# Two transformer blocks on one core: a new order of tables, a sixth place for weights, and the last expert's rows

## What is computed

```python
def first_block(x, p, positions, ...):
    h = x
    for i in range(DEPTH):                      # 2
        u = h @ w_in[i]
        y_mla = mla_mixer(...)                  # latent attention, rotary angles from positions
        y_diff = diff_mixer(...)                # softmax(q1 k1 + bias) - lam * softmax(q2 k2 + bias)
        y_sb = sb_mixer(...)
        h = layer_norm(ALPHA * h + concat(y_mla, y_diff, y_sb) @ w_o[i])
        ffn = grouped_moe(h, ...)               # 16 experts, two per token
        ple = sigmoid(h @ ple_gate[i]) * (p[i] @ ple_proj[i])
        h = layer_norm(ALPHA * h + ffn + ple)
    return h

def grouped_moe(h, ...):
    for e in range(16):
        hid = silu(h @ w_gate[e]) * (h @ w_up[e])
        out = out + gate[..., e:e + 1] * (hid @ w_down[e])

def diff_mixer(...):
    lam = exp(sum(lq1 * lk1)) - exp(sum(lq2 * lk2)) + lam_init
    bias = rel_bias[t5_bucket(rel)]             # from the distance of positions, 4 heads
    ...
```

## Time and profile before

| | before |
|---|---|
| runs | 2003.84 us median of 3 (2003.21 to 2006.06) |
| the profiled execution | 2008.08 us, its span 2006.8 us |
| mean granted clock of TensorE | 0.962 |
| busy share | PE 91%, weight load 78%, DVE 68%, ACT 57%, POOL 9% |
| chain that ended last | PE 67%, DVE 20%, ACT 6%, issue 2%, DMA 1% |
| bytes moved | 413.17 MB, mean 206 GB/s |

### The profile page before, as it was taken

The page is one execution under the profiler, slowest core; times in us unless marked ns, Lnnn a source line. Parts: engine busy times, 40 slices in busy tenths (PEclk is TensorE's granted clock), DMA queues, the critical chain, the costliest instruction groups (busy, mean ns, idle before and its releaser), DMA issues.

```text
span 2006.8 us, 27459 instructions
## 1 busy us (share of the span) xinstructions
PE 1825.2 (91%) x11220; PEld 1572.5 (78%) x11220; DVE 1363.4 (68%) x1591; ACT 1138.1 (57%) x1576; POOL 173.9 (9%) x152
## 2 busy tenths in 40 slices
PE   5978898999799889998878999989999999999998
PEld 4866777777587777776768889979898889988997
DVE  5576799899647579889875566565555556556555
ACT  4464588887636458878863644434444645434443
POOL 0000132311000003312110000000000000000000
PEclk9889899999889889999989999999999999999999
DMA  8314398999742348999884444645554544454552
GB/s 239 111 64 163 120 365 327 333 357 331 252 146 85 131 147 316 333 342 346 323 288 144 146 154 149 206 139 200 189 184 154 168 139 156 160 197 168 183 195 84
DMA packets 203011, 413.17 MB, mean 206 GB/s; under 512 B 16352, under 2 KB 118496, under 8 KB 186496
## 3 DMA queue, kind: packets, MB, share of 16 engines
q1 hardware_dynamic: 201792, 409.76, 59.2%
q10 hardware_dynamic: 1088, 1.57, 0.4%
HBM read 409.47 MB, written 1.84 MB: 205 GB/s over the span
## 4 chain that ended last, share of the span: by engine, by line
PE 67%; DVE 20%; ACT 6%; issue 2%; DMA 1%; POOL 0%; DVEq 0%; ACTq 0%
DVE weights_lo L389 12%; PE PS L404 9%; PE PS L408 9%; PE PS L405 9%; PE PS L412 7%; PE PS L415 6%; PE PS L416 6%; PE PS L1393 3%; PE PS L1396 3%; PE PS L1439 3%; PE PS L1418 3%; ACT weights_hi L384 2%; DMA arena<-in_w_down 1%; PE PS L1379 1%; DVE expert_rows_lo L1649 1%
## 5 line engine op out<-in xcount | busy, mean ns | idle before, releaser
L389 DVE TENSOR_TENSOR weights_lo<-weights_raw,weights_hi 128x1024 fp32r<-128x1024 f32 (+1 forms) x600 | 702.6, 1217 | 240.4 <-ACT weights_hi L384 238.0
L384 ACT ACTIVATE weights_hi<-weights_raw 128x1024 fp32r<-128x1024 f32 (+1 forms) x600 | 594.6, 1045 | 136.5 <-PE PS L416 84.4
L404 PE MATMUL PS<-hT_hi,weights_hi 128*128 128x256 f32 (+1 forms) x1488 | 428.6, 288 | 20.3 <-ACT weights_hi L384 11.4
L408 PE MATMUL PS<-hT_hi,weights_lo 128*128 128x256 f32 (+1 forms) x1488 | 425.8, 286 | 5.1 <-DVE weights_lo L389 5.1
L405 PE MATMUL PS<-hT_lo,weights_hi 128*128 128x256 f32 (+1 forms) x1488 | 425.4, 286 | 0.0
L404 PEld LDWEIGHTS PS<-hT_hi,weights_hi 128*128 128x128 f32 (+1 forms) x1488 | 285.9, 192 | 27.8 <-issue 14.5
L408 PEld LDWEIGHTS PS<-hT_hi,weights_lo 128*128 128x128 f32 (+1 forms) x1488 | 285.6, 192 | 6.9 <-DVE weights_lo L389 6.2
L405 PEld LDWEIGHTS PS<-hT_lo,weights_hi 128*128 128x128 f32 (+1 forms) x1488 | 286.0, 192 | 2.1
L412 PE MATMUL PS<-weights_hi,opa_hi 128*128 128x512 f32 x384 | 154.1, 401 | 8.3 <-DVE opa_lo L575 8.1
L415 PE MATMUL PS<-weights_lo,opa_hi 128*128 128x512 f32 x384 | 152.9, 398 | 0.0
L416 PE MATMUL PS<-weights_hi,opa_lo 128*128 128x512 f32 x384 | 152.8, 398 | 0.0
(11 more groups left out here) (322 smaller groups left out, 3203.3 us busy)
## 6 DMA issues: line engine op xcount, KB each, us to landing
weights_raw<-in_w_in SPq DMA_DIRECT2D x80, 1024.0 KB, 5.3
weights_raw<-in_w_ff SPq DMA_DIRECT2D x64, 1024.0 KB, 5.2
weights_raw<-in_w_up SPq DMA_DIRECT2D x42, 1024.0 KB, 7.1
weights_raw<-in_w_down SPq DMA_DIRECT2D x38, 1024.0 KB, 7.6
weights_raw<-in_w_gate SPq DMA_DIRECT2D x36, 1024.0 KB, 7.3
arena<-in_w_gate SPq DMA_DIRECT2D x14, 1024.0 KB, 7.0
params<-in_w_gate SPq DMA_DIRECT2D x14, 1024.0 KB, 7.0
arena<-in_w_down SPq DMA_DIRECT2D x14, 1024.0 KB, 7.7
```

The costliest lines, as they stand in the source:

```text
L384: act.activation(u.flat[0][:, c:e], u.x[:, c:e], ACT.Copy).then_inc(*sig.mark("w_hi", u.u, i))
L389: dve.tensor_tensor(u.flat[1][:, c:e], u.x[:, c:e], u.flat[0][:, c:e].bitcast(F32), ALU.subtract).then_inc(*sig.mark("w_lo", u.u, i))
L404: pe.matmul(o, w[0], x[0], start=start, stop=False)
L408: return pe.matmul(o, w[1], x[0], start=False, stop=stop)
```

## The change

1. **Places.** A sixth raw place, `mem(4096, UNIT)`, for units of experts from the ninth of each layer on. Late units so have five places, the others six. SP waits for `h and ple` ahead of its first use.

2. **Tables.** `small_sync` is split: lambdas' inputs stay ahead of mla 0, the other small loads and x go ahead of mla 1. The first sines move from behind bias 3 to behind bias 9, the first angles from bias 6 to bias 8, the second from behind the lambdas to bias 13. `red` has two buffers, so that DVE's angles don't alternate with ACT's sines; the sign goes in as the sine's scale. ACT's squares come ahead of the last bias steps, its second sines ahead of the lambdas' exponentials. On DVE the mask add comes right ahead of `diff_max`, the lambdas' difference behind it; the splits of `feed(sb q)` and `feed(sb k)` come one place later.

3. **Last expert.** In step 16 the turn comes ahead of the scatter of expert 14's second half, and the last expert's second half has rows of its own, `y_last`, in the space of `hT`; ACT's part of it no longer waits for the scatter of the first half.

```diff
                 late = of_expert(name) and not all(of_expert(n) for n, *_ in plan[u:u + 10])
-                n = NRAW if not of_expert(name) else NRAW + 1 if late else NRAW + 2
-                place = min(range(n), key=lambda i: -1 if last[i] is None else last[i])
+                allowed = list(range(NRAW)) + [NRAW] * (nth > 0) + [NRAW + 1] * (nth > 0 and not late) + [NRAW + 2] * (nth > 8)
+                place = min(allowed, key=lambda i: -1 if last[i] is None else last[i])
...
-        ang, turns, red = mem(2048, 256), mem(2304, 256), mem(2560, 256)
+        ang, turns, red = mem(2048, 256), mem(2304, 256), (mem(2560, 256), mem(2816, 256))
...
-                    act.activation(rope_tab[:, 2 * blk + part, :], red, ACT.Sin).then_inc(*sig.mark("tab_act", f"sine {blk}{part}"))
+                    act.activation(rope_tab[:, 2 * blk + part, :], red[part], ACT.Sin,
+                                   scale=col(COL_SIGN) if part else 1.0).then_inc(*sig.mark("tab_act", f"rope {blk}"))
...
                               landing16[:, i % 2, :, :]).then_inc(*sig.landing(f"bias_out{i % 2}", i))
+                if i == 9:
+                    sines(0)
                 yield
-                if i == 3:
-                    sines(0)
-                    yield
...
+            yield
+            sines(1)
             for l in range(DEPTH):
                 act.wait_ge(*sig.at("tab_dve", f"lambda sums {l}"))
                 act.activation(lam[:, l, 0:2], lam[:, l, 0:2], ACT.Exp).then_inc(*sig.mark("tab_act", f"lambda {l}"))
-            yield
-            sines(1)
...
-                if i == 6:
-                    angles(0)
+                if i in (8, 13):
+                    angles(i // 13)
...
+            dve.wait_ge(*sig.at("bias_in", "all"))
+            for k0 in (64, 320):
+                dve.tensor_tensor(bias8[0:64, :, k0:k0 + 64], bias8[0:64, :, k0:k0 + 64], bcast_mid(chunk_mask, 4),
+                                  ALU.add).then_inc(*sig.mark(c, "bias"))
+            yield
             for l in range(DEPTH):
                 dve.wait_ge(*sig.at("tab_act", f"lambda {l}"))
...
             diff_max(0, 0)
             diff_max(0, 1)
-            feed(n_("sb k"))
+            feed(n_("sb q"))
             diff_max(1, 0)
             diff_max(1, 1)
+            feed(n_("sb k"))
...
+            if l == 0:
+                dve.wait_ge(*sig.at("tab_dve", "lambdas"))
             diff_probs(0)
...
+        y_last = tuple(flat2(v)[:, 0:512] for v in hT)
+        def y_of(e_, half):
+            return y_last if (e_, half) == (N_EXP - 1, 1) else tuple(v[:, :] for v in y_e)
...
-                if e_ > 1:
+                if 1 < e_ < N_EXP:
                     add_to_tokens(e_ - 2, 1)
                 if e_ > 0:
                     turn_hidden(e_ - 1)
...
+                else:
+                    add_to_tokens(N_EXP - 2, 1)
                 if e_ > 0:
                     down(e_ - 1, 0)
...
-                act.wait_ge(*sig.at("ps", n_(f"add {e_} 0") if half else name))
+                act.wait_ge(*sig.at("ps", n_(f"add {e_} 0") if half and e_ < N_EXP - 1 else name))
...
             if name == "mla 0":
                 if l == 0:
-                    small_sync(sp)
+                    lambda_sync(sp)
                 up_params(sp, l)
+            if name == "mla 1" and l == 0:
+                small_sync(sp)
```

More of the change, by code:

```diff
@@ L374, in load_unit @@
                 l = int(u.name[-1])
-                sp.wait_ge(*(sig.at("ps", f"mla y {l}") if u.raw == NRAW else sig.at("norm_dve", f"ln1 {l} new1")))
+                sp.wait_ge(*(sig.at("ps", f"mla y {l}"), sig.at("norm_dve", f"ln1 {l} new1"),
+                             sig.at("moe_dve", f"h and ple {l}"))[u.raw - NRAW])
             sp.dma_start(u.x.rearrange("p (k n) -> p k n", k=u.k), plan[u.u][1]).then_inc(
@@ L785, in tables_vector @@
                 yield
-            dve.wait_ge(*sig.at("small_in", "all"))
+            dve.wait_ge(*sig.at("small_in", "lambda"))
             for l in range(DEPTH):
@@ L797, in tables_vector @@
                 dve.tensor_scalar(lam[:, l, 3:4], lam[:, l, 2:3], lam_init, None, ALU.add).then_inc(*sig.mark(c, "lambdas"))
-            yield
-            angles(1)
-            yield
-            dve.wait_ge(*sig.at("bias_in", "all"))
-            for k0 in (64, 320):
-                dve.tensor_tensor(bias8[0:64, :, k0:k0 + 64], bias8[0:64, :, k0:k0 + 64], bcast_mid(chunk_mask, 4),
-                                  ALU.add).then_inc(*sig.mark(c, "bias"))
         def tables_gpsimd(pool):
@@ L1029, in scalar_block1 @@
                 feed(n_(name))
-                take_steps(tables, 3 if name == "diff k0" else 2)
+                take_steps(tables, 2)
                 act.wait_ge(*sig.at("ps", n_(name)))
@@ L1049, in scalar_block1 @@
                 squares(act, crow[:, t, Q_RANK:], ms[:, 2 * t + 1:2 * t + 2], n_("mla squares"))
+            take_steps(tables, 5)
+            project_takes(act, feed, L("sb q"), "act_took", into(sqkT))
+            take_steps(tables, 1)
             if l == 0:
@@ L1438, in add_to_tokens @@
                     for part in range(2):
-                        last = pe.matmul(PS[:, 4 + 2 * t + half, :], from_slot[:, t * P:(t + 1) * P], y_e[part][:, :],
+                        last = pe.matmul(PS[:, 4 + 2 * t + half, :], from_slot[:, t * P:(t + 1) * P], y_of(e_, half)[part],
                                          start=e_ == 0 and part == 0, stop=e_ == N_EXP - 1 and part == 1)
```

57 lines of the change are left out of this document (27 added, 30 removed).

## The result

| | before | after |
|---|---|---|
| runs, first comparison | 2003.53 us median of 4 (2000.72 to 2006.06) | 1968.87 us median of 4 (1966.86 to 1972.56) |
| ratio, 95% interval | | 0.9829 [0.9808, 0.985] |
| the profiled execution | 2008.08 us, span 2006.8 | 1970.39 us, span 1969.1 |
| mean granted clock | 0.962 | 0.972 |
| busy share | PE 91%, DVE 68%, ACT 57% | PE 92%, DVE 69%, ACT 58% |

The kernel became faster by 34.7 us in the medians and by 37.7 us from one profiled execution to the other. The changed kernel was timed twice more beside experiments: 1969.35 us against 2006.28 (0.9818 [0.9804, 0.9831]) and 1968.66 us against 2003.05 (0.9833 [0.9818, 0.9847]). The forecast was 1965.1 us with a range of 1958 to 1977, and for the profiled execution 1969.4.

What follows compares the result with a forecast made beforehand. DVE's splits were taken to bound the experts' steady state. Tables 19.0 plus last expert 9.6 and 10.1 make 38.7 us; off the profiled 2008.08 that gives 1969.4, less 4.24 for the median 1965.1; range 1958 to 1977.

Steps and rivals of the forecast that it cites:

- Tables, 19.0 us forecast: First layer up to the second query tile's probabilities: two waits around the tables shrink, 19.0 us gained, bounds 12.2 to 22.
- The take at 36.9: ACT's take of diff k0, whose bank PE needs for bias 5: forecast at 36.9 instead of 47.30.
- the waits at bias 8 and 9: New PE waits for inputs that DVE makes behind its angle operations: forecast 1.45 and 1.5 us.
- the mask add that waits for the reload alone: DVE's mask add to the reloaded bias in the first layer: forecast at 83.9 instead of 102.97.
- Rival B: Tables give only 12 to 15 us, by later bias_out landings or a clock left at 0.50: 1969 to 1972; chance 0.19.
- Last expert, 9.6 and 10.1 us forecast: End of each layer's experts: earlier load, new order and upper clock gain 9.6 us in the first layer, 10.1 in the second.
- rival C: The last expert's loads land no sooner, 6 to 12 us less gain: 1971 to 1978; chance 0.13.
- The wait ahead of the first scatter: ACT's wait for down 15 0's load at the last expert: the load lands sooner, gaining 2.7 us.
- The clock step: Last expert: PE idles under 1 us at a time, so down's 16 matmuls take 3.75 instead of 6.1 us, gaining 2.4.
- Sixth place: Experts' steady state: DVE bounds it, so one more load under way changes nothing, 0 us.
- the 4.24 us: Last step of the sum: the old profiled execution exceeded its median by 4.24, taken off 1969.4 to give 1965.1.
- D: Rival with more gain: bias_out lands at its median and the clock stays whole, 1957 to 1961 us; chance 0.07.

Runs made afterwards that it cites:

- e2: The kernel before with the turn ahead of the second scatter and own rows for the last half, without the sixth place: 1991.83 us, ratio 0.9939.
- e3: The kernel before with the sixth place alone: 1994.91 us, ratio 0.9954.
- e9: The changed kernel with first sines, first angles and small loads back in their old places, the mask add still right behind the reload: 1979.23 us, ratio 0.9879.
- e6: The changed kernel with ACT's squares between bias 13 and 14 and the last half's own rows ahead of the next unit's split: 1967.79 us, ratio 0.9813.
- e11: The changed kernel with diff v1's load put off, squares between bias 13 and 14, own rows ahead of the next unit's split: 1966.49 us, ratio 0.9819.

## Why the prediction was right

**Tables, 19.0 us forecast.** A is 107.7 us in the mean of the three profiles of the changed kernel and 126.0 in the mean of the four with the old order of tables: 18.3 us. The take at 36.9, the waits at bias 8 and 9, and the mask add that waits for the reload alone are as worked out. Two terms were off and nearly cancel. The copy of bias 12 was put at 71.8 and starts at 69.8 in the mean of the three profiles (68.2 to 71.4). The way from it to the mask add was put at 12.1 us and takes 13.9, because the landing of bias_out 12 was taken as short as before, while in the new order it meets diff v1's load. So the mask add at 83.65 in the mean, where 83.9 was forecast, is in part luck. From there on 0.0 was forecast and it is 0.1 to 0.8 us more than before: PE's scores were taken to be ready by 82, and in two of the three profiles they come late, behind matmuls of sb q at the lower clock. Rival B named the right causes, bias_out among loads and the clock after a new wait (at bias 8 and 9 it fell in one of the three profiles, to 0.72 from 46.8 to 50.3), but mostly at the wrong bias steps, and priced them at 4 to 7 us where the sum lost under 1.

**Last expert, 9.6 and 10.1 us forecast.** B falls from 423.7 to 414.0 in the mean, C from 424.4 to 414.6: 9.7 and 9.8. The load is hardly waited for, which was rival C's question; the turns run at the upper clock; the last wait is 1.96 us, 0.4 and not 0.6 more than before. The wait ahead of the first scatter was to give 2.7 us and gave 2.6 in the first layer. The rest of the forecast, 5.1 + 2.4 - 0.6 = 6.9 us, is the way from the first scatter to the last, which is the same within 0.1 us in the three profiles of the changed kernel, 11.9 us in both layers, where the kernel before took 18.9 and 18.7. By itself the order takes 3.8 and 3.9 us of this way (e2) and the sixth place 1.0 and 2.7 (e3), less in sum than the 7.0 and 6.8 of both together.

The clock step was right for the whole change, but its reason, that PE stands still for less than 1 us at a time, was too simple: 1.13 us are left ahead of the scatter, and the clock stays up. With the order alone, 3.03 us ahead of the scatter bring the clock down (e2); with the sixth place alone, it falls behind several waits of 1.1 to 1.9 us (e3). Only with both do the turns take 1.89 us in both layers, and they do so in all nine profiles that have both.

**Sixth place.** 0 in the steady state, as forecast.

**The sum and the median.** 18.3 + 9.7 + 9.8 = 37.8 against 38.7; the profiled execution took 1970.39 where 1969.4 was said. The median came out 3.8 us above its forecast, 1968.87 against 1965.1. The step that failed here is the last: the 4.24 us between the profiled execution of before and its median were taken off the new kernel as well, where this difference is 1.5, and nothing in the second and third profile. A second profile of before was 1.8 us above the median of its comparison. So the 4.24 belonged to the execution, not to the kernel; with nothing taken off, 1969.4 us, the forecast would have been 0.5 us out. Where in an execution they come from stays open: from one profile of a kernel to the other A differs by up to 2.3 us, B by 1.8, C by 1.1 and the rest behind C by 3.7. The sum 37.8 is also more than the medians fell by in any of the three comparisons, 34.7, 36.9 and 34.4 us: in part this is because the waits were priced on an execution of before that was itself a long one, and the rest stays open.

**The range.** By the rivals' own bounds 1958 and 1977 are a little off: the middle of D is 1959, the far end of C 1978. The result is not near either.

## What to carry to other kernels

Where a step waits for something that has long arrived, read what stands ahead of it in its engine's program: moving the mask add in front of 10 us of work that nobody waited for, with the squares and the second sines and angles placed to suit, was worth 8 us (e9). Before moving loads or small transfers back and forth, list which large load is under way when a small one that is waited for is sent; a 1 MB load ahead of it made the landing 3.1 us here, once 4.7, instead of 1.7. And when an order at the end of a stage is changed for the clock's sake, count all idle times around it together: an order without gaps did not keep the clock up behind one of 3.03 us, and without the long gap the short ones were enough to lose it; the two changes together kept it.

## What was not expected of the hardware

The granted clock fell after 3.03 us of idle time although PE was busy without a break behind it (e2, 0.50 from 528.8 to 536.0), and before sb q it went either way behind the same waits: PE stood still for 1.55, 0.20 and 0.45 us in e6 and for 1.57, 0.20 and 0.43 us in e11. The stretch from 72.2 to 74.0 us, inside sb q, in e6 and in e11:

```profile
72.20:74.00 1.80, 1.72 (x8) 1.75 (x9) 1.67 (x8) 0.00 (x0) 0.47 (x1) 0.50 0.76 288
```

```profile
72.20:74.00 1.80, 1.80 (x18) 1.80 (x17) 1.63 (x10) 0.74 (x1) 0.88 (x1) 1.00 0.26 46
```

The granted clock is 0.50 in one and 1.00 in the other. The Trainium skill ("TensorE: Matmul & The Clock Gate", HAM oscillation — how this bites in real kernels) names idle gaps between matmuls as what takes the clock down. The first case agrees with it; the second shows the same waits in the same part of the program with and without a fall, and no run here shows what decides between them.

The small transfers of ACT's queue landed right behind a large load of SP's that had been issued before them: in the changed kernel's third profile in up to 3.1 us, in its second in up to 4.7, with that load put off in 1.7 at the most. The Trainium skill ("DMA: Bandwidth & Descriptors", Issuing engines are not separate DMA queues) says that transfers of different issuing engines run on the same 16 DMA engines and interleave. That a load of one queue holds up a transfer of the other is what the runs show (3.1 us against 1.7); of an interleaving that would let the small one through early these rows show little.
